# Second attention of a two-block model: fifteen phases to thirteen, probabilities scaled on VectorE

## The reference

```
s_cmp = qs @ k_cmp.T + bias_c ;  p_cmp = masked_softmax(s_cmp) ; o_cmp = p_cmp @ v_cmp
s_sel = qs @ k_slc.T + bias_s ;  p_sel = masked_softmax(s_sel) ; o_sel = p_sel @ v_slc
s_win = qs @ k_win.T + bias_w ;  p_win = masked_softmax(s_win) ; o_win = p_win @ v_win
out   = gc[0] * o_cmp + gc[1] * o_sel + gc[2] * o_win
```

## Time and profile before

| | us |
|---|---|
| median of 3 runs | 2774.45 |
| lowest and highest run | 2770.42, 2777.14 |
| profiled execution | 2776.2 |
| its span | 2774.1 |
| TensorE busy | 2721.2 (98%) |
| VectorE busy | 1945.3 (70%) |
| ScalarE busy | 1405.7 (51%) |

### The profile page before, as it was taken

The page is one execution under the profiler, slowest core; times in us unless marked ns, Lnnn a source line. Parts: engine busy times, 40 slices in busy tenths (PEclk is TensorE's granted clock), DMA queues, the critical chain, the costliest instruction groups (busy, mean ns, idle before and its releaser), DMA issues. The chain is left out here.

```text
span 2774.1 us, 41613 instructions
## 1 busy us (share of the span) xinstructions
PE 2721.2 (98%) x16606; PEld 2390.1 (86%) x16606; DVE 1945.3 (70%) x2922; ACT 1405.7 (51%) x2084; POOL 101.5 (4%) x189
## 2 busy tenths in 40 slices
PE   8999999999999999999999998999999999999998
PEld 7888888888888888888888898988888888888887
DVE  7448777757777775677656777876787775677765
ACT  6345555544455554455444551247655553455543
POOL 1320000000000000000000000000000000000000
PEclk9999999999999999999999999999999999999999
DMA  7457556655568878878656566762455556555554
GB/s 239 134 176 240 173 183 197 182 182 191 198 224 290 278 279 301 287 273 279 213 172 205 179 203 232 250 252 92 137 169 193 194 190 192 180 193 194 183 194 141
DMA packets 166609, 573.19 MB, mean 207 GB/s; under 512 B 19872, under 2 KB 26736, under 8 KB 165904
## 3 DMA queue, kind: packets, MB, share of 16 engines
q1 hardware_dynamic: 151216, 521.86, 56.7%
q0 software_dynamic: 15056, 48.65, 4.7%
q10 hardware_dynamic: 144, 0.01, 0.0%
HBM read 530.86 MB, written 38.90 MB: 205 GB/s over the span
## 5 line engine op out<-in xcount | busy, mean ns | idle before, releaser
L1911 DVE TENSOR_TENSOR wl<-raw,wh 128x1024 fp32r<-128x1024 f32 (+1 forms) x880 | 1029.1, 1195 | 449.2 <-ACT wh L1368 447.2
L1368 ACT ACTIVATE wh<-raw 128x1024 fp32r<-128x1024 f32 (+1 forms) x880 | 886.1, 1031 | 508.6 <-PE PS L947 417.0
L947 PE MATMUL PS<-CHt,wh 128*128 128x512 f32 x2816 | 887.2, 396 | 2.5 <-DVE wl L1911 2.5
L947 PE MATMUL PS<-BIGt,wh 128*128 128x512 f32 (+1 forms) x2816 | 757.9, 357 | 2.2 <-DVE wl L1911 1.2
L947 PEld LDWEIGHTS PS<-CHt,wl 128*128 128x128 f32 x2816 | 529.7, 188 | 125.0
L947 PE MATMUL PS<-AHt,wh 128*128 128x512 f32 (+1 forms) x1984 | 602.6, 385 | 12.5 <-DVE wl L1911 9.4
L947 PE MATMUL PS<-CHt,wl 128*128 128x256 f32 x2816 | 554.3, 278 | 0.0
L947 PEld LDWEIGHTS PS<-BIGt,wl 128*128 128x128 f32 x2304 | 436.2, 189 | 79.0 <-issue 0.2
L947 PE MATMUL PS<-BIGt,wl 128*128 128x256 f32 x2304 | 498.9, 279 | 0.0
L947 PEld LDWEIGHTS PS<-BIGt,wh 128*128 128x128 f32 x2816 | 436.4, 191 | 7.1 <-issue 4.4
L947 PEld LDWEIGHTS PS<-CHt,wh 128*128 128x128 f32 x2816 | 430.1, 189 | 3.0 <-issue 2.7
(11 more groups left out here) (307 smaller groups left out, 1647.1 us busy)
## 6 DMA issues: line engine op xcount, KB each, us to landing
raw<-in_w_up SPq DMA_DIRECT2D x264, 512.0 KB, 4.9
raw<-in_w_in SPq DMA_DIRECT2D x200, 512.0 KB, 4.1
raw<-in_w_down SPq DMA_DIRECT2D x132, 512.0 KB, 4.3
raw<-in_w_gate SPq DMA_DIRECT2D x88, 512.0 KB, 5.3
raw<-in_w_down SPq DMA_DIRECT2D x56, 384.0 KB, 3.6
raw<-in_w_ssd_br SPq DMA_DIRECT2D x32, 512.0 KB, 4.4
raw<-in_w_o SPq DMA_DIRECT2D x32, 512.0 KB, 4.4
PKR<-in_w_in SPq DMA_DIRECT2D x32, 512.0 KB, 5.4
```

What stands on the lines that cost most here:

```text
L947: return e.matmul(o, l, r, start=start, stop=stop, skip_group_check=True)
L1368: return e.activation(o, x, f, **k)
L1911: return e.tensor_tensor(o, x, y, op)
```

## The change

The scaling of the probabilities (`p0`, `p1`) goes from ScalarE to VectorE, right behind the reciprocals (`r0`, `r1`). The table of phases is written anew, with thirteen phases, in which the parts that read a TensorE or ScalarE result mostly stand one phase behind the part that makes it. Stage 3 gets two idle steps ahead, as stage 1 has. At the first half of a sub the plan now asks too whether bank 7 is held before it lets `ln` go on.

```diff
-ATTN2 = dict(sc0=0, cmp=2, tr0=5, o0=6, sc1=7, trc=10, oc=12, tr1=12, o1=14, s0=0, ca=2, r0=2, cb=5, s1=7, r1=9,
-             out=14, e0=2, ce=3, p0=3, t0=5, e1=9, tc=10, p1=10, t1=12)
+ATTN2 = dict(sc0=0, cmp=2, tr0=4, o0=6, sc1=6, trc=8, oc=10, tr1=10, o1=12, s0=1, ca=2, r0=3, cb=4, s1=7, r1=9,
+             out=12, e0=2, ce=3, t0=5, e1=8, tc=8, t1=11)
@@ all_units
-   gens=[attn2_stage(2 * i, 0), attn2_stage(2 * i + 1, 2 if i == 0 else 0)], **k)
+   gens=[attn2_stage(2 * i, 0), attn2_stage(2 * i + 1, 2 if i < 2 else 0)], **k)
@@ make_plan
-            if u.ev == "ev_add" or conv.live and conv.live[0][0] == "ln":
+            if u.ev == "ev_add" or conv.live and conv.live[0][0] == "ln" and not (
+                    len(conv.live[0][2]) > LN_END - 7 and bank7_taken()):
                 conv.step()
@@ TensorE, tr0 (tr1 the same with p13)
-                e.wait_ge(ac.sem, ac.at(i, "p03"))
+                e.wait_ge(d.sem, d.at(i, "p03"))
@@ ScalarE
-            def scale(br):
-                e.wait_ge(d.sem, d.at(i, f"rg{br}1"))
-                for hh in range(2):
-                    for b, c0, c1 in HALVES:
-                        x = SX[:, hh, c0:c1]
-                        af(x, x, ACT.Copy, scale=RC[:, hh, b:b + 1]).then_inc(ac.sem)
-            if ph == ATTN2["p0"]:
-                scale(0)
-            if ph == ATTN2["p1"]:
-                scale(1)
@@ VectorE, scale(br), behind the two products with the gates
+                e.wait_ge(d.sem, d.at(i, f"rg{br}1"))
+                for hh in range(2):
+                    for b, c0, c1 in HALVES:
+                        x = SX[:, hh, c0:c1]
+                        ts(x, x, RC[:, hh, b:b + 1], None, MUL).then_inc(d.sem)
```

More of the change, by code:

```diff
@@ L262, in all_units @@
                 k["banks"] = (0, 1)
-            add("w_in_2", 0, 16, 256 * i, "U2", "ev_q2", i,                 gens=[attn2_stage(2 * i, 0), attn2_stage(2 * i + 1, 2 if i == 0 else 0)], **k)
+            add("w_in_2", 0, 16, 256 * i, "U2", "ev_q2", i,                 gens=[attn2_stage(2 * i, 0), attn2_stage(2 * i + 1, 2 if i < 2 else 0)], **k)
         elif name == "x":
@@ L710, in hybrid_block_kernel @@
     a2_d = [steps(f"attn2_d{u}", "n000", "n010", "n100", "n110", "cb0", "cb1", "cm", "cs0", "cs1", "cf", "rc0", "rg00",
[L711 to L714, removed]
+                  "rg01", *[f"p0{j}" for j in range(4)], "cd", "cr", "cc", "cg0", "cg1", "cx0", "cx1", "n001", "n011", "n101", "n111", "rc1", "rg10",
+                  "rg11", *[f"p1{j}" for j in range(4)]) for u in range(2)]
+    a2_a = [steps(f"attn2_a{u}", *[f"e0{i}" for i in range(4)], "ce", "pt0", *[f"e1{i}" for i in range(4)], "ptc", "pt1") for u in range(2)]
     add_d = steps("conv_half_added")
@@ L1351, in attn2 @@
                 bank7("tr1")
-                e.wait_ge(ac.sem, ac.at(i, "p13"))
+                e.wait_ge(d.sem, d.at(i, "p13"))
                 turn()
```

## The result

The change costs time: 2782.53 us median of 6 runs (2781.79 to 2783.41), against 2773.95 (2770.42 to 2777.14) of the kernel before, run in turn with it. The ratio is 1.0030, 95% interval 1.0019 to 1.0040, or 8.6 us. The profiled execution took 2781.79 us, its span is 2780.0. The forecast was 2780.8, slower, in a range of 2766 to 2789.

The account below looks back on a forecast made before the run. TensorE, busy 98% of the span, was taken as the bound, so only its idle time and clock could move. Terms 5.05 + (10.9 - 11.3) + 0 + 0.9 + 0.8 = +6.35 us gave 2780.8 us, range 2766 to 2789.

Parts of the forecast that it names:

- `s0` behind the block: Stages 0, 2, 4: s0, one phase later, queues on VectorE behind convolution or layer norm; cmp waits about 2 to 3 us.
- Stages 0 and 1: From 1811 to 1852, beside the convolution: five new TensorE waits of 1.9, 1.0, 0.5, 0.65 and 1.0, sum 5.05 us.
- the walk: Following the three engines' queues through the second attention with per-instruction prices taken from the trace, to find TensorE's waits.
- Layer norm stretch: Stages 2 and 3 to stage 4's start: waits sum to 10.9 us against 11.3 before.
- Clock: Two slow spells again, 3.9 us, so net 0; bounds none and three. The no-change rival, 2776.9 to 2778.9, had 0.22.
- Stages 4 to 7: trc of the odd stage waits behind s1, 0.45 us for each of two pairs: 0.9; bounds none and 3.
- End: Attention ends five steps earlier, so its last values no longer cover the add of H: 0.8 us.
- Price of a group: One scaling group on VectorE costs 0.95 us, with bounds of 0.70 and 1.15.
- the rule on the doubled mode: VectorE ops with one source, destination in SBUF and even outermost dimensions run doubled: group 0.95 us, without it 1.15.
- The rival named backlog: Slower still: late s0 delays splits, stages 4 to 7 lose 3, third slow spell: +11.4, 2785.9 us; chance 0.10.
- three signs of being wrong: TensorE idle below 3 us in stages 0 and 1, below 6 in the layer norm stretch, or clock 1.00 throughout.
- The rival named relief: Faster: ScalarE's 5.6 us were what the layer norm stretch lacked; -2.9, or -8 (2766.5 us) with VectorE slack; chance 0.20.

Follow-up runs that it names:

- the scaling alone: Kernel before, old fifteen phases, with only the scaling moved from ScalarE to VectorE: 2774.79 us, +0.1 over before.
- the plan alone: Changed kernel's thirteen-phase table, later stage 3 and bank 7 test, with the scaling left on ScalarE: 2786.82 us, +12.1 over before.
- the convolution's swap: Changed kernel with the attention's phase planned ahead of the convolution's blocks only, layer norm's blocks staying ahead: 2781.51 us, +7.0 over before.
- swapping the order within the step: Changed kernel, table untouched, with the attention's phase planned ahead of convolution and layer norm blocks in quick subs: 2775.53 us, +1.2 over before.
- the last variant: Kernel before with layer norm phases 7 to 12 behind the attention's phase, three idle steps among them, and only p1's scaling on VectorE: 2767.34 us, -7.2.
- the kernel with `s0` back: Changed kernel with s0 put back from phase 1 to phase 0, the phase of sc0: 2781.84 us, +7.1 over before.
- the one with the last pair later: Kernel with s0 back at phase 0, and stages 6 and 7 begun four and five steps later: 2783.30 us, +8.6 over before.

## Why the prediction was right, and where not

*The step "`s0` behind the block".* Right. The timeline of VectorE after shows it for stages 0 and 2: a run of twelve convolution taps, which is two blocks, and only then `s0`; and the eight subtractions of the layer norm, and only then `s0`. Before, `s0` stood between the blocks and ahead of the subtractions.

```profile
1810.54 4.84 DVE L1908 SCALAR_TENSOR_TENSOR CC<-Z,CV,CC 128x256 f32<-128x256 f32 x12
1815.29 0.30 DVE L2525 CUSTOM_DVE_ANT_0 SX2a<-PS,BM 128x128 f32<-128x128 f32 x1
...
1857.09 2.77 DVE L1900 TENSOR_TENSOR CC<-CC,TA 128x256 f32<-128x256 f32 x8
1859.78 0.28 DVE L2525 CUSTOM_DVE_ANT_0 SX2a<-PS,BM 128x128 f32<-128x128 f32 x1
```

The Trainium skill ("Perfetto Trace Analysis", Tensor Engine Instruction) calls VectorE and ScalarE strict FIFO; these rows agree: the scores of stage 0 were done at 1811.6 (1810.69 + 0.93 in TensorE's timeline above), and `s0` ran 3.7 us later, behind the blocks.

*Stages 0 and 1: +5.05 of waits predicted, 3.4 measured.* The waits of 1.9, 0.65 and 1.0 are there (1.87, 0.55, 0.97). The 1.0 at `tr0` of stage 0 and the 0.5 at `cmp` of stage 1 are not. VectorE isn't the reason: its scaling ended at 1821.99, and by the walk, moved to this execution (1.65 us earlier), at 1821.95. TensorE came 1.4 us later than the walk has it (1822.35 for 1820.95), since its clock was 0.50 to 0.68 in the four microseconds from 1817 to 1821. The transposes in TensorE's timeline, without a wait:

```profile
1822.35 0.82 PE L1283 MATMUL PS<-M,SX2a 128*128 128x128 f32 x6
```

So the spell took up waits of 1.5 us, and the two together are what the walk had: from the first product of stage 0 to that of stage 2 the kernel after needs 42.05 us (1810.69 to 1852.74), the kernel before 36.89 (1812.34 to 1849.23), 5.2 more.

*Layer norm stretch: -0.4 predicted, -0.5 measured* (10.8 us of waits, for 10.9 by the walk). The 2.8 was 3.01, the 2.5 of stage 4 was 3.77. The small ones (0.85, 0.35, 1.6) came as 1.20, 0.55 and 1.02, and the 2.8 at `o1` was 1.22. So two of the sizes were off by more than 1 us in opposite ways, and that the sum fits is partly luck. `PT2a,VC` doesn't wait any more, as the prediction said.

*Clock: 0 predicted, about 3.4 us measured.* This is the term that was mis-sized, though its bounds ("none and three" spells) were meant to hold it; there are four. I took the waits of 2.5 and more as those that bring the low level. The wait of 1.87 already did, and the waits of 1.20 and 1.02 around 1884 to 1888 had one too.

*Stages 4 to 7: +0.9 predicted, 2.5 measured*, in six small waits. The walk found one place per pair; the scaling, the add of `H` and `s1` meet at more.

*End: +0.8 predicted, 1.11 measured*, and it is the add of `H`.

*Price of a group: 0.95 predicted.* The groups of instructions after have 0.283 and 0.348 us for the two shapes, and a group of four is 0.92 from its first start to the next instruction's (1821.07 to 1821.99):

```profile
L1904 DVE TENSOR_SCALAR SX2b<-SX2b,SM 128x256 f32<-128x256 f32 x16 | 5.6, 348 | 0.0
L1904 DVE TENSOR_SCALAR SX2a<-SX2a,SM 128x128 f32<-128x128 f32 x16 | 4.5, 283 | 0.3
```

The 0.065 us for 128 more columns is the pace of the rows without a pointer (0.139 for 256). So the rule on the doubled mode in the Trainium skill ("VectorE: DVE Perf Modes", What auto-detection actually checks), which the prediction weighed, fits these tiles with a pointer too. The prediction's upper bound of 1.15 was mis-added: by its own steps it is 2 x (0.329 + 0.19) = 1.04. The forecast doesn't use it; the rival named backlog does, for a term of 1 us.

*Sum.* Waits: +6.35 predicted, +6.5 measured. Clock: +3.4 beside it. The result is +8.6 by medians; the forecast was right in sign and cause and short by the clock's part. That the waits agree to 0.15 us is luck: stages 0 and 1 came 1.65 below the walk (mostly the spell), stages 4 to 7 came 1.6 above it.

*The signs.* The waits ahead of `KDC,Q` at stages 0, 2 and 4 came, 1.87 to 3.77 us for "about 2 to 3"; so did the 64 new instructions and the absence of a wait ahead of `PT2a,VC`. Idle time in the first window was to be about 6 us and was 3.5. None of the three signs of being wrong came, the first by 0.5 us. The rival named relief fell with the scaling alone (+0.1): its argument, that ScalarE names the two largest waits and is the busier engine there, is refuted for the old phases by the 3.55 and 3.05 that stay. In the new plan the move does relieve, by the 3.5 us between the plan alone and the change, less than the plan costs.

Open: what decides on a slow spell, and how long it lasts. It is not the waits alone, as the last section shows. So the 0.86 behind the convolution's swap, against 0.89 without it, is no more than two executions with equal waits differ by (0.96 and 0.92 above), and the price of the clock in one trace is not the price in the median.

## What to carry to other kernels

When every engine runs one written order, "one phase behind the producer" is no fixed distance: look at what else stands between the two in the reader's own queue, and put short readers that TensorE waits for ahead of long blocks that nobody waits for. Moving one reader alone hands the wait to the next; swapping the order within the step removed most of it. And an engine named by a wait need not be relieved by taking work from it when that work goes to the partner of the same chain: moved whole, ahead of the layer norm's tiles, the scaling cost 2.6 us there; half of it, with the layer norm spread, gained 3. Whether the half or the spread made that difference is not shown: the whole scaling with the layer norm spread was not run.

## What the runs showed of the hardware

A slow spell doesn't follow the length of the last wait. In the kernel after a wait of 1.87 us, 4 us behind one of 1.39, was followed by a clock of 0.72 (1818 to 1823 above). The same waits needn't bring the same clock either. The kernel before and the last variant have waits of 1.17 (1.16), 1.22 (1.23) and 2.12 us at the same places of the same plan; behind the 2.12 the kernel before stays at 2.4 GHz, and the variant falls to the 1.2 GHz level. The windows of the kernel before and then of the variant:

```profile
1872.00:1877.00 5.00, 4.83 (x44) 4.40 (x46) 4.20 (x19) 3.92 (x8) 0.00 (x0) 1.00 0.01 3
```

```profile
1872.00:1877.00 5.00, 5.00 (x36) 4.61 (x34) 2.74 (x12) 4.49 (x12) 0.00 (x0) 0.66 0.14 20
```

In the kernel with `s0` back, windows behind its wait of 2.20 and over its later waits of 2.29 and 2.88:

```profile
1864.00:1872.00 8.00, 8.00 (x44) 7.50 (x46) 5.11 (x25) 4.28 (x10) 0.00 (x0) 0.57 0.22 80
1895.00:1905.00 10.00, 6.73 (x70) 5.75 (x70) 5.36 (x11) 6.85 (x14) 0.00 (x0) 1.00 0.17 54
```

2.20 us brought close to the 1.2 GHz level for eight microseconds; 2.29 and 2.88 left the clock at 2.4 GHz, and behind them too (1.00 from 1900 to 1976). An earlier wait of 2.29 in the same execution, which ended at 1881.58, did bring the low level (0.57 from 1881 to 1889). And behind the wait of 3.44 in stage 0, with the same plan up to there, the low level lasted four microseconds in that kernel (1823 to 1827, after the wait, which ended at 1822.03) and eight in the one with the last pair later (1823 to 1831, begun within the wait, which ended at 1824.72).
